# Operands of 512 columns (high and low part) in 118 slabs a layer, and look-up of picks by equality tests on 2-byte values

## The reference, cut to what matters

```python
# mixer
z = h @ w_in                    # 3584 columns: xin, b, c, q, k, v, o, and 8 gate columns
...                             # short conv on c*xin; mLSTM on q, k, v; both gated
x = x + concatenate([y_conv, y_lstm]) @ w_out
# cross-attention: q = h @ w_xq, k and v from the normalised memory, 4 heads of 256
# expert network, 8 heads, 2 x 128 keys, 16384 experts of one neuron
q = (xb @ w_pq).reshape(128, 8, 2, 128)
sc = einsum('thpc,hpkc->thpk', q, sub_keys)
sv, si = top_k(sc, 16)                              # 16 best rows, 16 best columns
cand = sv[..., 0, :, None] + sv[..., 1, None, :]    # 256 sums
fv, fi = top_k(cand, 16)                            # 16 best sums
eid = si row * 128 + si column of each pick
g = softmax(fv)
a = gelu(einsum('thkd,td->thk', u_experts[eid], xb))
out = einsum('thk,thkd->td', g * a, v_experts[eid])
```

## Time and profile before

| | |
|---|---|
| median of 3 runs | 2184.36 us (2181.97 to 2188.09) |
| profiled execution, its own time | 2184.32 us |
| its span in the trace | 2182.7 us |
| TensorE busy | 2127.6 us, 97% of the span |
| TensorE weight loads busy | 1975.6 us, 91% |
| VectorE busy | 1580.2 us, 72% |
| ScalarE busy | 1098.5 us, 50% |
| GpSimd busy | 343.3 us, 16% |
| mean granted TensorE clock | 0.993 |
| moved by DMA | 437.49 MB, mean 200 GB/s |

### The profile page before, as it was taken

The page is one execution under the profiler, slowest core; times in us unless marked ns, Lnnn a source line. Parts: engine busy times, 40 slices in busy tenths (PEclk is TensorE's granted clock), DMA queues, the critical chain, the costliest instruction groups (busy, mean ns, idle before and its releaser), DMA issues. The chain is left out here.

```text
span 2182.7 us, 47685 instructions
## 1 busy us (share of the span) xinstructions
PE 2127.6 (97%) x15224; PEld 1975.6 (91%) x15224; DVE 1580.2 (72%) x2591; ACT 1098.5 (50%) x1651; POOL 343.3 (16%) x344
## 2 busy tenths in 40 slices
PE   6999999999999999999989999999999999999998
PEld 6999899999999888888789989999999998888886
DVE  6665658998777676677675746599977776767776
ACT  6445454444455555555464545444455554555554
POOL 3110110000000143344230101100000003333331
PEclk9999999999999999999999999999999999999999
DMA  5444466765555777777634454566655557777775
GB/s 188 156 151 154 146 203 216 228 205 184 182 182 181 244 251 240 241 241 240 225 127 155 148 167 166 185 228 229 201 182 180 180 180 264 242 240 241 241 240 165
DMA packets 173982, 437.49 MB, mean 200 GB/s; under 512 B 19360, under 2 KB 84896, under 8 KB 172752
## 3 DMA queue, kind: packets, MB, share of 16 engines
q1 hardware_dynamic: 173232, 432.09, 60.7%
q0 software_dynamic: 672, 4.39, 0.6%
HBM read 399.70 MB, written 36.70 MB: 200 GB/s over the span
## 5 line engine op out<-in xcount | busy, mean ns | idle before, releaser
L750 DVE TENSOR_TENSOR w_lo<-raw,w_hi 128x1024 fp32r<-128x1024 f32 x680 | 842.1, 1241 | 406.9 <-ACT w_hi L718 193.9
L1152 PE MATMUL ps<-act_hi,w_hi 128*128 128x256 f32 x2880 | 830.6, 288 | 3.2 <-DVE act_lo L801 1.9
L1152 PE MATMUL ps<-act_hi,w_lo 128*128 128x256 f32 x2880 | 816.9, 284 | 0.0
L1152 PE MATMUL ps<-act_lo,w_hi 128*128 128x256 f32 x2880 | 816.2, 283 | 0.0
L1152 PEld LDWEIGHTS ps<-act_hi,w_hi 128*128 128x128 f32 x2880 | 554.1, 192 | 5.2 <-issue 2.3
L1152 PEld LDWEIGHTS ps<-act_hi,w_lo 128*128 128x128 f32 x2880 | 554.5, 193 | 0.1
L1152 PEld LDWEIGHTS ps<-act_lo,w_hi 128*128 128x128 f32 x2880 | 554.3, 192 | 0.0
L718 ACT ACTIVATE w_hi<-raw 128x1024 fp32r<-128x1024 f32 x248 | 263.1, 1061 | 324.0 <-PE ps L1412 311.5
L1412 PE MATMUL ps<-w_hi,act_hi 128*128 128x512 f32 x1000 | 389.2, 389 | 1.8 <-DVE act_lo L1116 1.8
L1412 PE MATMUL ps<-w_lo,act_hi 128*128 128x512 f32 x1000 | 389.0, 389 | 0.0
L1412 PE MATMUL ps<-w_hi,act_lo 128*128 128x512 f32 x1000 | 389.0, 389 | 0.0
(11 more groups left out here) (249 smaller groups left out, 2060.0 us busy)
## 6 DMA issues: line engine op xcount, KB each, us to landing
raw<-slabs SPq DMA_DIRECT2D x684, 512.0 KB, 3.7
h_park<-h_out SPq DMA_DIRECT2D x256, 128.0 KB, 1.7
h_in<-h_park SPq DMA_DIRECT2D x250, 128.0 KB, 3.9
memT<-mem POOLq DMA_DIRECT2D x2, 1024.0 KB, 6.9
skT<-sub_keys POOLq DMA_DIRECT2D x2, 1024.0 KB, 7.1
x_park<-xT SPq DMA_DIRECT2D x2, 1024.0 KB, 5.3
xT<-x_park SPq DMA_DIRECT2D x2, 1024.0 KB, 8.5
xT<-x SPq DMA_DIRECT2D x1, 1024.0 KB, 4.9
```

Of the source, the lines that this page charges most:

```text
L750: nc.vector.tensor_tensor(w_lo[:, j].rearrange("p k c -> p (k c)"), raw[:, j, :], w_hi[:, j].rearrange("p k c -> p (k c)").bitcast(FP32), ...
L1152: last = nc.tensor.matmul(ps[:, j, 0:T], w[:, j, k, :], a[:, k, :], start=(k == 0 and i == 0), stop=(k == KB - 1 and i == 2))
```

## The change

The change has two parts.

**Wide operands.** `act_hi` and `act_lo` become the two halves of one tensor `act_2`, `pre_hi` and `pre_lo` those of `pre_2`; their places in memory stay. `wide_product` multiplies `w_hi` with both halves at once, 512 columns in two blocks of 256, into the whole PSUM bank, and `w_lo` with the high half, 256 columns, into its first half. A slab then has 16 matmuls. The columns 0 to 255 hold two of the three products, the columns 256 to 511 the third, and somebody has to add them. It is used for 28 + 8 + 16 slabs of Z, Q and PQ and for the `u` slabs 58 to 123, 118 a layer. The others stay narrow.

- In Z, Q and PQ ScalarE copies the second half to `zT`, `qT` or `qpT` (`half_out`), and VectorE adds the first half to it and then counts `act_evac`.
- The `kT` results, which ScalarE copied, are copied by VectorE (`k_group`).
- In the hot stage ScalarE copies the second half to `h_out` (`half_of`), VectorE adds the first (`add_u`, after `hot_rows`), and ScalarE takes the Gelu in place (`gelu_of`), after the copy of the gates.

**Look-up of picks.** The rank of the row is now computed by shifts and maxima, so that both look-ups are equality tests. Each is 16 fused instructions (compare with the constant a, multiply by key a) of 256 values each, written as 2-byte values, and a tree of four additions. `cand_at` and `top_d` go.

```diff
+            def wide_product(j, a, before=None):
+
+                for k in range(KB):
+                    if before is not None:
+                        before(k)
+                    nc.tensor.matmul(ps[:, j, :], w_hi[:, j, k, :], a[:, :, k, :], start=(k == 0), stop=False)
+                    last = nc.tensor.matmul(ps[:, j, 0:T], w_lo[:, j, k, :], a[:, 0, k, :], start=False, stop=(k == KB - 1))
+                last.then_inc(slab_done, 1)
...
             def copy_to(dst, first=0):
-                return lambda j, n: nc.scalar.activation(dst[:, ds(n + first, 1), :], ps[:, j:j + 1, 0:T], ACT.Copy)
+                return lambda j, n: nc.scalar.activation(dst[:, ds(n + first, 1), :], ps[:, j:j + 1, T:2 * T], ACT.Copy)
...
+            def add_half(layer, dst, j, n, half):
+
+                dve.wait_ge(half_out, layer * HALVES + half + n + 1)
+                nc.vector.tensor_tensor(dst[:, ds(n, 1), :], dst[:, ds(n, 1), :], ps[:, j:j + 1, 0:T],
+                                        ALU.add).then_inc(act_evac, 1)
+
+            def z_group(layer, at0, slots=range(RING)):
+                for j in slots:
+                    add_half(layer, zT, j, at0 + j, 0)
+                    lo_part(layer, at0 + RING, 0, j)
+
+            def k_group(layer, at0, first, slots=range(RING)):
+                for j in slots:
+                    dve.wait_ge(slab_done, layer * SLABS + at0 + j + 1)
+                    nc.vector.tensor_copy(kT[:, first + j:first + j + 1, :], ps[:, j:j + 1, 0:T]).then_inc(act_evac, 1)
+                    lo_part(layer, at0 + RING, 0, j)
...
+                def half_of(at0, g, j):
+
+                    act.wait_ge(slab_done, layer * SLABS + U_AT + at0 + g * RING + j + 1)
+                    act.wait_ge(h_stored[j % H_SLOTS], (layer * (U_SLABS // H_SLOTS) + at0 // 2 + g * 2 + j // 2) * 16 + 16)
+                    nc.scalar.activation(h_out[:, j % H_SLOTS:j % H_SLOTS + 1, :], ps[:, j:j + 1, T:2 * T],
+                                         ACT.Copy).then_inc(u_half, 1)
+
+                    act.wait_ge(raw_loaded[j], (layer * (SLABS // RING) + ((U_AT + at0) // RING + 2) + g) * 16)
+                    nc.scalar.activation(w_hi[:, j].rearrange("p k c -> p (k c)"), raw[:, j, :],
+                                         ACT.Copy).then_inc(hi_ready, 1)
+
+                def gelu_of(at0, g, j):
+                    slot = h_out[:, j % H_SLOTS:j % H_SLOTS + 1, :]
+                    act.wait_ge(u_sum, layer * WIDE + at0 - WIDE_AT + g * RING + j + 1)
+                    nc.scalar.activation(slot, slot, ACT.Gelu).then_inc(act_evac, 1)
...
+                def add_u(n, j):
+                    slot = h_out[:, j % H_SLOTS:j % H_SLOTS + 1, :]
+                    dve.wait_ge(u_half, layer * WIDE + n + (HOT_AT - WIDE_AT + j + 1))
+                    nc.vector.tensor_tensor(slot, slot, ps[:, j % RING:j % RING + 1, 0:T], ALU.add).then_inc(u_sum, 1)
+
                 with dve.Fori(0, GROUPS // RING) as g:
                     for j in range(RING):
                         hot_rows(g * RING + j)
+                        add_u(g * RING, j - 2)
                         lo_part(layer, U_AT + HOT_AT + (j + 2) // RING * RING, g, (j + 2) % RING)
...
+                step.mark(nc.vector.tensor_scalar(by16_u[:], flat_i, 4, None, ALU.logical_shift_right))
+                step.mark(nc.vector.tensor_scalar(by8_u[:], flat_i, 3, None, ALU.logical_shift_right))
...
+                step.mark(nc.vector.scalar_tensor_tensor(a_f[:], by8_u[:], -2.0, by16_u[:], ALU.add, ALU.max))
...
+                for side, (place, found) in enumerate(((a_at, row_f), (b_at, col_f))):
                     step.join()
+                    for a in range(TOPK):
+                        step.mark(nc.vector.scalar_tensor_tensor(
+                            pick[:, a], place[:].rearrange("p (c k) -> p c k", k=TOPK), float(a),
+                            keys[:, :, side, a].unsqueeze(2).to_broadcast([P, TB * PH, TOPK]), ALU.is_equal, ALU.mult))
+                        spend(0.45)
+                    n = TOPK // 2
+                    while n:
+                        step.join()
+                        out = found[:].rearrange("p (o c k) -> p o c k", o=1, k=TOPK) if n == 1 else pick[:, 0:n]
+                        step.mark(nc.vector.tensor_tensor(out, pick[:, 0:n], pick[:, n:2 * n], ALU.add))
+                        spend(0.13 * n + 0.2)
+                        n //= 2
```

More of the change, by code:

```diff
@@ L866, in _ @@
                 last.then_inc(arg_ready, 1)
[L867 removed]
+                z_group(layer, Z_O, (2, 3))
                 dve.wait_ge(dw_ready, layer + 1)
@@ L873, in _ @@
                 nc.vector.memset(u_pad[:, :, 0:2], 0.0)
-                group(layer, Z_B)
+                z_group(layer, Z_B)
                 dve.wait_ge(qk_mm, layer + 1)
@@ L879, in _ @@
                 last.then_inc(s_ready, 1)
-                group(layer, Z_U)
+                z_group(layer, Z_U)
                 dve.wait_ge(nd_mm, layer + 1)
@@ L913, in _ @@
                     step.link(last)
-                group(layer, Z_C, (2, 3))
+                z_group(layer, Z_C, (2, 3))
                 dve.wait_ge(hr_mm, layer + 1)
@@ L928, in _ @@
                 operand_lo(layer, USE_XATTN)
-                group(layer, K2_AT)
-                section(layer, Q_AT, Q_SLABS)
+                k_group(layer, K2_AT, 4)
+                section(layer, Q_AT, Q_SLABS, qT, Q_HALF)
                 blocks = [slice(b * XH, (b + 1) * XH) for b in range(TB)]
@@ L952, in _ @@
                 norm(xT, par[:, G_FFN:G_FFN + 8], layer * NORMS + NORM_FFN + 1, to_xn, rstd_pre)
-                group(layer, PQ_AT)
+                for j in range(RING):
+                    add_half(layer, qpT, j, j, PQ_HALF)
+                    lo_part(layer, PQ_AT + RING, 0, j)
                 operand_lo(layer, USE_FFN)
-                section(layer, PQ_AT + RING, PQ_SLABS - RING)
+                section(layer, PQ_AT + RING, PQ_SLABS - RING, qpT, PQ_HALF, RING)
                 due = [RING, 0.0]
@@ L1170, in group, with wide_group @@
                     slab_product(j, hi, lo, before if j == 0 else None)
+            def wide_group(layer, at0, ev_at, a=act_2, slots=range(RING), before=None):
+                for j in slots:
+                    pe.wait_ge(lo_ready[j], lo_count(layer, at0, 0))
+                    pe.wait_ge(act_evac, layer * ACT_EVS + ev_at + j + 1)
+                    wide_product(j, a, before if j == 0 else None)
             def mean_square(layer, at0):
@@ L1246, in _ @@
                 last.then_inc(v_tr, 1)
-                group(layer, Z_B, Z_B)
+                wide_group(layer, Z_B, Z_B)
                 pe.wait_ge(arg_ready, layer + 1)
@@ L1255, in _ @@
                 last.then_inc(qk_mm, 1)
-                group(layer, Z_U, Z_U)
+                wide_group(layer, Z_U, Z_U)
                 pe.wait_ge(s_ready, layer + 1)
@@ L1381, in _ @@
                 last.then_inc(ret_mm, 1)
-                group(layer, U_AT + at, U_EV + at, slots=range(RET_AT % RING, RING))
+                wide_group(layer, U_AT + at, U_EV + at, slots=range(RET_AT % RING, RING))
                 def gates_of(n, s):
```

159 lines of the change are left out of this document (77 added, 82 removed).

## The result

The changed kernel takes 2166.0 us (median of 6 runs, 2160.0 to 2170.6) against 2184.7 for the kernel before beside it (6 runs, 2182.0 to 2189.6): ratio 0.9906, 95% interval 0.9893 to 0.9920. A second series of 5 runs gave 2165.9 us and 0.9914 (0.9900 to 0.9927). The forecast was 2162.9 us in a range of 2148 to 2177: the sign, the size and the range held, and the time was 3.1 us above it. It lies where the forecast's own range (2156 to 2166) ends and that of rival D (2166 to 2176) begins. The profiled execution took 2166.97 us (span 2165.3).

The account below looks back on a forecast made before the run. It took TensorE's issue cadence plus a few waits as the bound. From 2184.3 us it took 14.1 for wide slabs net of losses and 7.3 for the decode, giving 2162.9 us, 8-in-10 range 2148 to 2177.

Parts of the forecast that it names:

- rival D: Wide slabs' tails double, with more waits in Z and more time at 1.2 GHz: 2166 to 2176 us; chance 0.12.
- hot stage and tail, 66 wide slabs a layer: Hot stage: TensorE's period falls from 3.62 to 3.51 us a round; 13.9 us gained.
- Z at full clock, 28 wide slabs a layer: Z stages: wide slabs save 0.105 us each, less 3.7 us for longer `e_row` waits; 2.2 us gained.
- Q and PQ, less the waits at their ends: Q and PQ: wide slabs' savings less 2.0 us of longer waits for the last evacuations; 3.0 us gained.
- clock in Z: Z: a longer stretch at the lower clock after the longer `e_row` wait; 1 us lost.
- decode: wait gone: Look-up of picks: TensorE's 3.6 us wait a layer goes, with a smaller one-hot wait following; 7.3 us gained.
- decode: clock: Stretch after the look-up's wait: what the clock gives back was taken as not earned; 0 us.
- slabs that give no share: 27 slabs ahead of TensorE waits or at 1.2 GHz, whose faster products gain nothing; 2.8 us taken off.
- TensorE's cadence: Slab products: 2.775 us wide against 2.880 narrow, as each matmul pays a price per instruction; 0.105 us less a slab.
- Rival A: Wide operands: the break between the two blocks eats the gain; 2180 to 2184.9 us, no change; chance 0.11.
- Rival B: Hot stage becomes VectorE's, deciding from 3.62 us a round; at 3.97 us a round, 2222 us; chance 0.08.
- Tails: Two-step evacuation not hidden: 2.0 us after Q and PQ, 3.7 at `e_row`, 1.2 at `kT`, lost in all.

Follow-up runs that it names:

- kernel 5: The changed kernel with Z's slabs narrow again and `kT` copied by ScalarE; Q, PQ and hot stage stay wide: 2157.8 us, ratio 0.9875.
- kernel 3: The changed kernel with Z, Q and PQ narrow again and `kT` copied by ScalarE; only the hot stage stays wide: 2161.9 us, ratio 0.9885.
- kernel 4: The changed kernel with `act_2` and `pre_2` laid out so that the 512 columns are one contiguous run: 2164.1 us, ratio 0.9899.
- kernel 2: The changed kernel with the old look-up of picks, so the wide operands alone: 2178.2 us, ratio 0.9952.
- kernel 1: The kernel before with the new look-up of picks alone, all slabs narrow: 2176.3 us, ratio 0.9958.
- kernel 8: The changed kernel with two more 256-column additions on VectorE in each hot-stage round, never read: 2231.2 us, ratio 1.0214.
- kernel 10: The changed kernel with the 12 one-column products dealt out over the first slab of Z_C: 2165.0 us, ratio 0.9905.
- kernel 6: The changed kernel with Z_B, Z_U and Z_C narrow, their banks copied out by VectorE: 2164.4 us, ratio 0.9907.
- kernel 11: kernel 5 with the 12 one-column products dealt out over the first slab of Z_C: 2158.4 us, ratio 0.9882.
- kernel 7: kernel 5 with 36 never-read constant products on TensorE ahead of the wait for `pre` at the layer's start: 2166.8 us, ratio 0.9913.

## Why the prediction was right, step by step

The terms, in us for both layers. The right column is from stage lengths as above (`kT` and Q are parted at the sum of squares behind the output projection); the clock's in Z is half of the difference in time at 1.2 GHz.

```
step of the prediction                       forecast   measured
hot stage and tail, 66 wide slabs a layer      13.9       10.3
Z at full clock, 28 wide slabs a layer          2.2        3.6
Q and PQ, less the waits at their ends          3.0        2.9
kT to VectorE                                  -1.2       -1.0
clock in Z                                     -1         -5.1
decode: wait gone                               7.3        7.5
decode: clock                                   0          1.1
turn of the layer                               -         -1.0
```

(Forecast of Z: 56 x 0.105 less the 3.7 for `e_row`. The 2.8 us of slabs that give no share, which the prediction took off as one term, belong to these rows; with them the left column makes 21.4. The right column sums to 18.3. With 0.6 more in the expert output, 0.5 more ahead of the first slab and 0.1 less in the scores it makes the 17.3 us between the two profiled executions. The medians are 18.7 and 19.0 apart.)

That the total came within 3.1 us is luck in part. The hot stage brought 3.6 us less than its term, the clock in Z took 4.1 more and the turn of the layer 1.0; against that stand 1.4 us more from Z, 1.1 us of clock at the look-up, and the 2.8 us that were taken off ahead. Rival D, "the tails double: more waits in Z, more time at 1.2 GHz", came true in its second half: the time at 1.2 GHz grew, while the waits at the tails cost about what was forecast. The result lies at its edge.


- **TensorE's cadence: right.** The pair was put at 0.2269 + 0.1200 us. In Q it is 0.230 + 0.117 (medians of the starts), so 2.77 us a slab against the forecast's 2.775; kernel 5 against kernel 3, both without `cand_at`, shows the same fall from 2.88 in Q. Rival A is refuted by that and by kernel 4. The price per instruction of the Trainium skill (TensorE: Matmul & The Clock Gate, "Wait — 56ns, not 53.3ns?"), 2.5 ns beside the columns, would have made it 0.020 us a slab. The runs have 0.105 in Q and 0.080 in the hot stage, so the trace does not agree in size for these operands. Nor is the price one number: the narrow slabs of `mem` pay 0.0101 us a matmul beside the columns where those of `act` pay 0.0133 (2.80 and 2.88 us a slab).
- **Q and PQ: right by luck.** Of the 2.9 us some 1.0 is the gain with the 64 bytes (0.31 a layer in the key slabs ahead of Q, 0.20 in PQ). The wide slabs' own part is 1.9 (kernel 2 against kernel 1 in layer 0: 36.66 less 36.49 and 80.12 less 79.33, twice), less than forecast: the waits for `qT` and `qpT` grew by 2.8 us in all instead of 2.0.
- **Hot stage, mis-sized.** "Period falls from 3.62 to 3.51" was 3.54: 5.05 us in 63 rounds, not 6.6. The prediction took the narrow slab there at Q's 0.1200 a matmul, but the first matmuls behind the one-hots started 0.118 apart in the kernel before, and the wide pair takes 0.349 there instead of 0.347. The stage is the largest, so this is the largest miss that the clock doesn't make: 3.6 us.
- **Rival B was nearer than 8% said.** It decides at VectorE's round against TensorE's. The prediction had 3.42 to 3.57 for the one; kernel 8 gives 3.38, 0.16 us under the other. The right side by 5% of a round.
- **Tails.** `qT` and `qpT`: 0.5 us each forecast, 0.6 to 0.7 measured. `kT`: 1.2 forecast, 1.0 against the kernel before, 1.7 against kernel 5. `e_row`: 3.7 forecast, 0.6 measured, 1.9 in kernel 2. Its end moved from 66.71 to 67.65 us, by 0.9 where five adds were to make 1.9. The five adds took 1.7 us of VectorE's queue, but the eight passes over `memT` took 0.5 us less than before and the four `w_lo` ahead of them 0.4 less; why is open. Nor is the 0.6 what the longer queue costs TensorE, for it waited differently in the two layers. Its wait for `e_row` in layer 0 and in layer 1, and windows of 4 us some 13 us ahead of each:

```profile
PE ps L1307 <- DVE e_row L902: 0.6, 1, 0.6
PE ps L1307 <- DVE e_row L902: 2.1, 1, 2.1
```

```profile
54.00:58.00 4.00, 4.00 (x16) 0.60 0.73 248
1126.00:1130.00 4.00, 4.00 (x25) 1.00 0.71 246
```

  In layer 0 the clock had fallen in the V slabs, TensorE came later, and 1.5 us of the wait were gone. It is so in all five layers with a wide Z_K to Z_O and such a fall (0.6 us each); in the nine without one the wait is 2.0 to 2.2 us, and with a narrow Z 1.0 to 1.1 in all twelve. So five adds cost TensorE 1.0 to 1.2 us a layer at full clock, and a slow stretch ahead of this wait costs next to nothing.
- **The clock, the step that failed in kind.** The prediction had 1 us "after the longer `e_row` wait". With a wide Z, 27.3 us of the two Z stages ran at 1.2 GHz in the changed kernel (both times) and in kernel 10, 30.7 in kernel 2 and 34.1 in kernel 4, and 23.9 in kernel 6, with its last slabs narrow; with a narrow Z it was 17.1 (before and kernel 1), 20.5 (kernels 3 and 5) and 13.7 (kernel 11). Half of the difference is 3 to 10 us, against the 3.6 that the slabs gain there at full speed over the kernel before (1.4 to 1.8 over the kernels 3, 5 and 11). It is not a law of wide slabs: kernel 8, with a wide Z, had 17.1, and kernel 7, with a narrow one and the filler, 27.3. The prediction's step, a longer stretch after a longer `e_row` wait, is borne out by itself: behind the nine waits of 2.0 to 2.2 us the clock was low for 6.8 us eight times and for 3.4 once, behind the twelve of 1.0 to 1.1 us for 6.8 three times, for 3.4 seven times and not at all twice. What it had not counted is the block of one-column products, behind which all of the changed kernel's extra 10.2 us lie, in both of its executions. The runs did not show what makes the rest of the stretches. Each execution draws its own (the same binary went from 2155.8 at a granted clock of 0.997 to 2162.0 at 0.993 in kernel 5), and what is shown is a mean over few profiles.
- **Decode: right.** The wait is gone and 1.2 us of `hot_row` stand in its place (forecast 1.5). VectorE ended with `g_exp` at 478.6 us and TensorE came for it at 481.98, 3.4 us later, so the look-up has room to spare. "What the clock gives back is not earned" was wrong by 1.1 us: the stretch after the wait had cost that.
- **Turn of the layer.** No step had it: 1.0 us more between the layers. It is not scatter: the turn takes 7.2 to 7.8 us in the six traces with all of Z wide, and 6.0 to 6.5 in the six others without filler. ScalarE's first instruction there stood behind 3.65 us of its own issue, 2.35 in kernel 5 and 2.66 in kernel 6. Why is open.

The best version of those tried is kernel 5, with 2157.8 us: new look-up, wide slabs in Q, PQ and the hot stage, narrow ones in Z, `kT` with ScalarE.

## What to carry to other kernels

Fewer, longer matmuls are worth their count times the price of an instruction, and that price is to be read from the cadence of two sizes in the trace, in the stage where it counts and with the operand that it has there: here it changed for operands that had moved by 64 bytes. Take them where TensorE streams without a stop; in a stage with short waits, an evacuation in two steps lengthened those for `e_row`, `kT`, `qT` and `qpT` by 0.7 to 1.2 us a layer each, and the gain was small or lost. When a change removes a tensor, compare a stage that the change does not touch: it may have moved too. An engine's margin in a loop is its own round against the other's, not its idle time: part of that is issue and can't be filled.

## What the runs showed of the hardware

- An operand of 512 columns in two runs of 256, 8 KB apart, streams as fast as one run (223.01 and 223.02 us for 63 rounds).
- A matmul of 512 columns took 0.227 us from start to start among its like and 0.230 to 0.232 with a 256-column neighbour, and that neighbour 0.117 instead of 0.120.
- Narrow slabs of the same 24 matmuls took 2.88 us with the moving operand where the kernel before has it and 2.80 with it 64 bytes lower, in 3 and 10 traces. In kernel 8 it lies 2 KB higher again, and the slabs take 2.80.
- A fall of the clock some 13 us ahead of a wait cost nearly nothing: the wait for `e_row` shrank from 2.1 to 0.6 us (5 of 5 layers).
- The clock fell to 1.2 GHz for 3.4 us behind each 3.6 us wait for `g_exp` (4 of 4), and behind a block of one-column matmuls, with TensorE busy without a gap, in all 8 layers of the changed kernel (twice), kernel 2 and kernel 4, in 5 of 6 of kernels 5, 6 and 7, and in none of the 8 of the kernel before and kernels 1, 3 and 8. Dealt out among long matmuls, the same instructions let it fall in 0 of 4, two of these in a kernel with a wide Z.
